# Order of the last two residual tiles on ScalarE, VectorE and GpSimd in a one-layer trunk step

## The reference

```
x = x + g1 * rmsnorm(t, lp['g_post1'])
h = rmsnorm(x, lp['g_pre2']) * (1 + sc2) + sh2
aff = softmax(h @ w_router)                  # 16 experts
vals, idx = top_k(aff.swapaxes(1, 2), cap)   # 64 latent and 16 context tokens per expert
xs = h[idx]                                  # the rows that each expert works on
```

## Time and profile before

| | us |
|---|---|
| median of three runs | 2847.84 |
| profiled execution | 2848.99 |
| its span in the trace | 2847.4 |
| PE busy | 2791.4 |
| VectorE busy | 2106.8 |
| ScalarE busy | 1502.7 |
| GpSimd busy | 282.0 |

### The profile page before, as it was taken

The page is one execution under the profiler, slowest core; times in us unless marked ns, Lnnn a source line. Parts: engine busy times, 40 slices in busy tenths (PEclk is TensorE's granted clock), DMA queues, the critical chain, the costliest instruction groups (busy, mean ns, idle before and its releaser), DMA issues.

```text
span 2847.4 us, 40931 instructions
## 1 busy us (share of the span) xinstructions
PE 2791.4 (98%) x15008; PEld 2390.7 (84%) x15008; DVE 2106.8 (74%) x1918; ACT 1502.7 (53%) x1466; POOL 282.0 (10%) x337
## 2 busy tenths in 40 slices
PE   7999999999999999999999997999999999999998
PEld 5688888899999999999988776888888888888886
DVE  2339788796777777763344577888888888888888
ACT  4411221125556566552233455777777777777776
POOL 1000000002111111100000001001010101100100
PEclk9999999999999999999999997999999999999999
DMA  9877667664343443364343767999999999999997
GB/s 370 311 266 255 228 252 265 224 227 135 120 123 119 123 123 123 102 207 124 123 143 119 292 215 276 356 402 395 395 398 389 396 393 397 391 388 387 392 394 297
DMA packets 258406, 757.23 MB, mean 266 GB/s; under 512 B 20249, under 2 KB 127297, under 8 KB 194001
## 3 DMA queue, kind: packets, MB, share of 16 engines
q1 hardware_dynamic: 234272, 650.01, 61.3%
q0 software_dynamic: 23120, 100.71, 10.9%
q10 hardware_dynamic: 928, 5.33, 0.5%
HBM read 700.61 MB, written 55.37 MB: 265 GB/s over the span
## 4 chain that ended last, share of the span: by engine, by line
PE 91%; DVE 3%; DMA 2%; ACT 1%; issue 1%; DVEq 0%; ACTq 0%; SPq 0%; POOL 0%; POOLq 0%
PE ps L542 21%; PE ps L544 21%; PE ps L543 21%; PE ps L2402 5%; PE ps L2403 5%; PE ps L2404 5%; PE ps L2569 3%; PE ps L2571 3%; PE ps L2570 3%; PE ps L2259 2%; PE ps L2507 1%; DMA raw<-in_w_mod 1%; DVE rsd L1827 1%; PE ps L2282 1%; DVE xc L1649 0%
## 5 line engine op out<-in xcount | busy, mean ns | idle before, releaser
L467 DVE TENSOR_TENSOR we_lo<-raw,we_hi 128x2048 fp32r<-128x2048 f32 x384 | 877.5, 2290 | 114.0 <-ACT we_hi L462 113.8
L462 ACT ACTIVATE we_hi<-raw 128x2048 fp32r<-128x2048 f32 x384 | 736.9, 1920 | 261.4 <-PE ps L544 261.4
L411 ACT ACTIVATE w_hi<-raw 128x2048 fp32r<-128x2048 f32 x115 | 220.1, 1914 | 444.3 <-PE ps L544 356.5
L421 DVE TENSOR_TENSOR w_lo<-raw,w_hi 128x2048 fp32r<-128x2048 f32 x115 | 263.5, 2291 | 192.4 <-ACT w_hi L411 187.8
L542 PE MATMUL ps<-we_hi,xs_lo 128*128 128x512 f32 x1024 | 399.7, 390 | 0.1
L544 PE MATMUL ps<-we_hi,xs_hi 128*128 128x512 f32 x1024 | 399.3, 390 | 0.0
L543 PE MATMUL ps<-we_lo,xs_hi 128*128 128x512 f32 x1024 | 399.3, 390 | 0.0
L2402 PE MATMUL ps<-hi,w_lo 128*128 128x320 f32 x1152 | 365.3, 317 | 0.9 <-ACT stage L1122 0.9
L2403 PE MATMUL ps<-lo,w_hi 128*128 128x320 f32 x1152 | 355.9, 309 | 0.0
L2404 PE MATMUL ps<-hi,w_hi 128*128 128x320 f32 x1152 | 355.8, 309 | 0.0
L1614 DVE SCALAR_TENSOR_TENSOR mod_acc<-mod_raw,sc,mod_acc 128x2048 f32<-128x2048 f32 x120 | 276.7, 2348 | 3.3
(11 more groups left out here) (447 smaller groups left out, 4772.0 us busy)
## 6 DMA issues: line engine op xcount, KB each, us to landing
raw<-in_w_e_gate SPq DMA_DIRECT2D x128, 1024.0 KB, 8.0
raw<-in_w_e_up SPq DMA_DIRECT2D x128, 1024.0 KB, 7.5
raw<-in_w_e_down SPq DMA_DIRECT2D x128, 1024.0 KB, 12.1
raw<-in_w_in SPq DMA_DIRECT2D x144, 512.0 KB, 5.7
mod_raw<-in_w_mod SPq DMA_DIRECT2D x64, 1024.0 KB, 5.3
raw<-in_w_mod SPq DMA_DIRECT2D x64, 512.0 KB, 7.6
raw<-in_w_o SPq DMA_DIRECT2D x64, 512.0 KB, 4.9
d_proj<-g_stage POOLq DMA_DIRECT2D x32, 320.0 KB, 2.4
```

Of the source, the lines that this page charges most:

```text
L411: act.activation(w_hi[:, j % NHL, s], raw[:, slot, s], ACT.Copy).then_inc(hi_ready, 1 if fine else 2)
L421: dve.tensor_tensor(w_lo[:, j % NHL, s], raw[:, slot, s], w_hi[:, j % NHL, s].bitcast(F32), ALU.subtract).then_inc(lo_ready, 1 if fine else 2)
L462: act.activation(we_hi[:, k % NEH, :], raw_slot(k), ACT.Copy).then_inc(hi_ready, 2)
L467: TTn(we_lo[:, k % NEH, :], raw_slot(k), we_hi[:, k % NEH, :].bitcast(F32), ALU.subtract).then_inc(lo_ready, 2)
```

## The change

For tiles 0 and 1 alone. ScalarE copies the turned blocks of a tile ahead of its square, and writes the unread squares into the input buffer `x_t` instead of `h2`. For tile 0 VectorE multiplies by the norm weights first, without 1/rms, and then scales by 1/rms and adds the shift in one instruction. For tile 1 the product with the norm weights is GpSimd's, the scaling by 1/rms ScalarE's, the shift GpSimd's as before. The logit rows are copied by VectorE instead of ScalarE. Two more semaphore names are taken from earlier ones.

```diff
+                 "h2_product": ("cols_taken", 4), "h2_scaled": ("small_act", 4)}
@@ gpsimd
+            pool.wait_ge(S["x2_ready"], 7)
+            pool.wait_ge(S["shift_loaded"], 32)
+            pool.wait_ge(S["h2_stored0"], 2 * 16)
+            pool.tensor_tensor(even_odd(h2[:, 0, :]), by_parity(t_out[:, 1, :]), by_parity(VL[:, 1, :]), ALU.mult
+                               ).then_inc(S["h2_product"], 1)
             pool.wait_ge(S["h2_ready"], 4)
             store_h2(3)
             pool.wait_ge(S["affT_taken"], 4)
+            wait(pool, "h2_scaled", 1)
             pool.tensor_tensor(even_odd(h2[:, 0, :]), even_odd(h2[:, 0, :]), by_parity(shift[:]), ALU.add
@@ scalar: square
-                if q >= 2:
-                    act.wait_ge(S[f"h2_stored{q % 2}"], q // 2 * 16)
-                own.done(act.activation(h2[:, q % 2, :], t_out[:, t, :], ACT.Square, accum_out=stats[:, 48 + t:49 + t]))
+                if q == 2:
+                    act.wait_ge(S["h2_stored0"], 16)
+                unread = h2[:, q % 2, :] if q < 3 else x_t[:, q % 2, :]
+                own.done(act.activation(unread, t_out[:, t, :], ACT.Square, accum_out=stats[:, 48 + t:49 + t]))
@@ scalar
+            take_x2(3, (4, 5, 0, 1))
             square(3)
-            take_x2(3, (4, 5, 0, 1))
+            take_x2(4, (2, 3, 4, 5), 1)
             square(4)
-            take_x2(4, (2, 3, 4, 5), 1)
-            act.wait_ge(S["logit_done"], 4)
-            act.activation(logit_rows[:], ps[:, 6, 0:2 * P], ACT.Copy).then_inc(S["x2T_taken"], 1)
...
+            wait(act, "h2_product", 1)
+            act.activation(h2[:, 0, :], h2[:, 0, :], ACT.Identity, scale=stats[:, 57:58]).then_inc(S["h2_scaled"], 1)
@@ vector: last_affinities
+                own.settle()
                 dve.wait_ge(S["logit_done"], 5)
@@ vector
             take_first()
-            second_scale(3)
-            second_shift(3)
-            second_scale(4)
+            dve.wait_ge(S["h2_stored1"], 16)
+            h = even_odd(h2[:, 1, :])
+            own.done(TTn(h, by_parity(t_out[:, 0, :]), by_parity(VL[:, 1, :]), ALU.mult))
+            dve.wait_ge(S["x2_sqrt"], 4)
+            own.done(dve.reciprocal(stats[:, 56:57], stats[:, 48:49]))
+            own.settle()
+            STT(h, h, stats[:, 56:57], by_parity(shift[:]), ALU.mult, ALU.add).then_inc(S["h2_ready"], 1)
+            dve.wait_ge(S["logit_done"], 4)
+            dve.tensor_copy(logit_rows[:], ps[:, 6, 0:2 * P]).then_inc(S["x2T_dve"], 1)
+            dve.wait_ge(S["x2_sqrt"], 5)
+            own.done(dve.reciprocal(stats[:, 57:58], stats[:, 49:50]))
             last_affinities()
@@ tensor: router_pair
-                pe.wait_ge(S["x2T_taken"], 20)
+                pe.wait_ge(S["x2T_dve"], 2)
```

More of the change, by code:

```diff
@@ L369, in trunk @@
                  "spread_set": ("hid_done", 2 * NE + 1), "y2_summed": ("hidT_done", 2 * NE + 2 * (TT - 1)),
-                 "gates_hi": ("row_act", 8), "gates_lo": ("small_dve", 2)}
+                 "gates_hi": ("row_act", 8), "gates_lo": ("small_dve", 2),
+                 "h2_product": ("cols_taken", 4), "h2_scaled": ("small_act", 4)}
         for name, (early, _) in LATER.items():
```

## The result

| | before | after |
|---|---|---|
| median, 17 runs each | 2847.84 (2846.60 to 2850.27) | 2853.92 (2851.92 to 2857.46) |
| profiled execution, us | 2848.99 | 2854.12 |
| its span | 2847.4 | 2852.5 |

The ratio of after to before is 1.0021, 95% interval 1.0015 to 1.0028: slower by 6.1 us (4.3 to 8.0), where 2.7 us were forecast. The time is above the range of the prediction, which ended at 2852.6. The direction and the mechanism of the wait held, the size did not.

A forecast was written before the change was run, and what follows sets the result against it. The chain to the logit copy, ahead of the first expert matmul, was taken as the bound; the wait for GpSimd swallows ScalarE's 2.45 us, +2.7 on 2848.99 is 2851.7, less 1.15 for the median: 2850.5, range 2845.2 to 2852.6.

The forecast's parts named there:

- What bounds the stretch: Between last output-projection and first expert matmul, 1693 to 1736 us: only when the logit copy ends counts.
- ScalarE's order: Block copies ahead of squares: last copies end 2.45 us earlier, router done at about 1705.4 instead of 1707.88.
- The wait for GpSimd's product: VectorE's tile 0 product waits 4.1 us for GpSimd's; logit copy ends at 1711.0, 2.7 us later than before.
- rival C: VectorE's and GpSimd's products share, each at part speed; VectorE loses 2.05 us, total 2848.6; chance 0.13.
- Clock: PE's low clock level at the start of the expert stage: nothing in the sum, up to 1.2 us either way.
- Tile 1's rows: Scaling on ScalarE, add on GpSimd from 1713.05 instead of 1712.84: nothing added to the end, 3.08 us of slack.
- rival D: GpSimd's second add becomes the bound, adding 1.5 us and a further 1.2 by the clock: 2853.2; chance 0.05.
- A shift reaches the end one for one: Expert stage: PE busy for 95.00 of 95.00 us, so a later start delays the kernel's end by the same time.
- From the profiled execution to the median: Whole kernel: the median of before's runs lies 1.15 us under the profiled execution, so 2851.7 becomes 2850.5.
- The range: Whole kernel's median: 2845.2 to 2852.6 us, leaving out outcomes given a chance of 0.08.
- A: The forecast case: VectorE's product waits for GpSimd's; 2850.5 us, own range 2849.0 to 2852.0; chance 0.46.
- The sign: Whole kernel: slower, by 2.7 us.

The follow-up runs named there:

- e3: The kernel before with only ScalarE's new order, block copies ahead of squares, and the squares written to x_t; 2849.89 us, ratio to before 1.0008.
- e14: The kernel before with ScalarE's block copies ahead of the squares, which still go to h2; 2847.43 us, one execution.
- e2: The changed kernel with GpSimd's product replaced by three memsets, which write and don't read; 2848.91 us, ratio to before 1.0003.
- e6: The changed kernel with GpSimd's product also waiting for tile 0's root, so that VectorE's product starts first; 2854.17 us, one execution.
- e7: The changed kernel with GpSimd's product over plain contiguous rows instead of even columns ahead of odd; 2854.30 us, one execution.
- e5: Against the changed kernel: VectorE makes both products, ScalarE both scalings, GpSimd both adds beside the top-8, tile 0 stored from ScalarE's queue; 2852.26 us, ratio to before 1.0012.
- e8: The kernel before with two more 128x2048 products on VectorE ahead of the last affinities, a pure delay; 2852.66 us against 2848.41, ratio 1.0016.
- e12: The kernel before with 8 more one-column activations on ScalarE ahead of the expert loop; 2848.72 us, ratio to before 1.0000.
- e17: The kernel before with the squares of tiles 0 and 1 written to x_t, nothing else; 2846.61 us, one execution.
- e1: The changed kernel with GpSimd's product of tile 1 moved behind the store of tile 0; 2853.47 us, ratio to before 1.0018.
- e4: e1 with the logit copy between VectorE's product and its scale-and-shift, and the first gather issued ahead of GpSimd's memsets; 2852.75 us, ratio to before 1.0017.
- e9: e5 with the eighth weight load of expert 0 held until the store of tile 1 has landed; 2848.43 us, ratio to before 0.9999.
- e13: The kernel before with squares written to x_t and the waits for h2's stores in VectorE's list, not ScalarE's; 2849.94 us, one execution.
- e16: The kernel before with two more waits, for h2's stores, in VectorE's list alone; 2848.21 us, one execution.

## Why the prediction was wrong, point by point

- *What bounds the stretch*: right. The chain runs over the logit copy and everything in the stretch behind it moved along.
- *ScalarE's order*: right. The router is done at 1704.87, forecast 1705.4; 0.4 of this is the clock, since its last 24 matmuls took 1.60 us and the 2.03 of before had been carried over. That this gains nothing by itself (e3, e14) was only half seen: the slack of VectorE was counted, its need of 1/rms was not, since in the changed kernel it is gone.
- *The wait for GpSimd's product*: the mechanism was right (7.21 us, e2, e6), and rival C's sharing is refuted, since the engine that comes second does next to nothing until the first is done. The term was mis-sized. I had taken 4.59 us from an add in which one input is strided, for a product in which both are: it takes 5.49 (e7: 4.57 when contiguous). So VectorE's product was 7.21 instead of 6.4, and the logit copy ended at 1711.58 instead of 1711.0. 3.26 us in place of 2.7.
- *Clock*: "nothing in the sum" was the choice, and it came out near that: +0.36 at the turns of `xs`, and 0.50 given back in the first expert. Its bound of 1.2 either way is about right. Up to the first expert's next turns of `xs` the traces range from 44.8 (e5) to 46.5 us (e2), by the clock.
- *Tile 1's rows*: right. The second add kept 4.58 us beside the top-8, the gather was released by the index with 2.85 us to spare, and rival D did not come.
- *A shift reaches the end one for one*: this is the step that failed. The windows of before showed PE busy for 95.00 of 95.00 us, and from this I took it that a loop with unchanged instructions would keep its length. For a pure delay it does (e8). In after PE waits for VectorE in the first expert and in every second step of the loop, and the part behind the first expert matmul is 1.6 us longer, the clock aside. Nothing in the windows of before said that it can be, and why it is stays open.
- Of the 2.4 us between the 2.7 forecast and the 5.1 of the profiled executions this makes 1.6, the strided product 0.6, the later landing of the gather 0.3, and the clock -0.1.
- *From the profiled execution to the median*: the prediction took off 1.15 us, as before's profiled execution lies above its median. After's lies 0.20 above its own. These 0.95 us are the rest, from 5.1 to 6.1, and they are within the interval of 4.3 to 8.0. Only profiled executions have a trace, so their cause is not shown. The traces do show that before's was a long one: from the first residual half to the end it took 1151.1 us, e12 and e17, which have the same work and steps of 67.42, 1149.6 and 1149.7.
- *The range*: its top, 2852.6, is not worked out from the terms. A with the clock gives 2851.7, and A's own range ended at 2852.0. It left no room for a term that no row had shown. The sign was right by the rule of the Trainium skill named in the prediction; had I asked which other VectorE instructions it names, I could have seen before e1 that moving the product need not help.

## What to carry to other kernels

In these runs GpSimd arithmetic that reads SBUF was free beside VectorE's top-8, and cost its whole remaining length beside a product of two SBUF tensors or a small `tensor_scalar`. List what VectorE runs in the whole time of GpSimd's instruction, and look at the kind of each, down to two elements a row: one of them on the critical path pays for all of GpSimd's work. And a transfer that is moved later meets others: e5 won 2.2 us in the stretch and lost 4.6 because a freed buffer let a load start beside the last store. Last, that PE is busy throughout a loop before a change does not say that the loop keeps its length: compare its steps in both traces.

## What the runs showed of the hardware

- A `tensor_scalar` over 128x2 took 4.59 and 5.65 us while GpSimd read SBUF, 0.17 otherwise (e1, e4). The top-8 instructions, a PSUM-fed one and a reduce beside GpSimd's reads were not longer.
- A GpSimd product of 128x2048 took 5.42 to 5.49 us with both inputs at every second column, 4.57 contiguous (e7), and its add with one strided input 4.58. The Trainium skill, GPSIMD Engine Reference, section "Performance pitfalls for Q7 kernels", has the slower reading begin at steps above 8 bytes; here the step is 8 bytes. The measurement decides: with two such inputs there is a price of 0.92 us (e7, one execution).
- A 1 MB store took 4.2 us to land, and 8.1 beside a 1 MB load issued 0.9 us ahead of it (e9, e5).
- VectorE's product of two SBUF tensors kept its 2.29 us beside three GpSimd memsets of 128x2048, which only write, and took 7.21 behind a GpSimd product begun 0.43 us ahead of it (e2, after).
- The same loop took 67.40 to 67.65 us in its second step, depending on what stood ahead of it in the program.
- The same stretch took 12.63 to 13.58 us by PE's clock: 24 router matmuls took 1.60, 2.03, 2.39 or 2.76 us and four logit matmuls 0.59 or 1.00, in kernels with the same work there (before, e12, e13, e16, e17).
